# A hybrid encoder block with routed experts on one core: gates read sooner, first gathers spaced, exponentials moved, and VectorE making more low parts

## The reference

```python
def one_block(x_blk):                              # 128 tokens
    q = (x_blk @ w_q).reshape(n, 8, 2, 128)
    s = einsum('nhpc,hpkc->nhpk', q, keys32)
    top_s, top_i = lax.top_k(s, 16)                # 16 of 128 keys, twice
    ...                                            # best 16 of their 16 x 16 sums
    expert_idx = take_along_axis(cand_i, best_c)
    gate = softmax(best_s)
    act = gelu(einsum('nhkd,nd->nhk', expert_u[expert_idx], x_blk))
    return einsum('nhk,nhkd->nd', gate * act, expert_v[expert_idx])
```

## Time and profile before

| what | us |
|---|---|
| median of three runs | 1655.65 |
| the profiled execution | 1660.05 |
| its span | 1658.3 |
| TensorE busy | 1621.8 (98%) |
| VectorE busy | 1288.4 (78%) |
| ScalarE busy | 790.8 (48%) |
| GpSimd busy | 776.4 (47%) |
| granted TensorE clock, mean | 0.996 |
| DMA, mean over the span | 285 GB/s |

### The profile page before, as it was taken

How to read it: one execution, slowest core, us unless ns; L and a number is a source line. 1 busy time by engine, 2 the same in 40 slices (tenths; PEclk the granted TensorE clock), 3 DMA queues, 4 the chain that set the end, 5 groups by cost and what they waited for, 6 DMA issues and landing times.

```text
span 1658.3 us, 26242 instructions
## 1 busy us (share of the span) xinstructions
PE 1621.8 (98%) x10068; PEld 1449.7 (87%) x10068; DVE 1288.4 (78%) x2091; ACT 790.8 (48%) x938; POOL 776.4 (47%) x498
## 2 busy tenths in 40 slices
PE   7999999999998999999999999989999999999998
PEld 6877778889998999999999999988888888888886
DVE  3666622265999989999799689766788998989897
ACT  6454433336554566667667667633323233332323
POOL 4333334446855464444455555433365534453450
PEclk9999999999999999999999999999999999999999
DMA  5222223425649999999999999997999999999993
GB/s 165 77 76 76 76 77 90 121 81 141 191 122 355 379 377 317 345 342 331 356 354 407 417 353 409 386 323 249 362 358 396 395 396 396 395 396 395 396 393 134
DMA packets 247527, 472.81 MB, mean 285 GB/s; under 512 B 13824, under 2 KB 169504, under 8 KB 242080
## 3 DMA queue, kind: packets, MB, share of 16 engines
q1 hardware_dynamic: 173520, 253.52, 43.4%
q0 software_dynamic: 55296, 201.35, 31.6%
q10 hardware_dynamic: 18640, 17.06, 3.0%
HBM read 427.84 MB, written 44.04 MB: 285 GB/s over the span
## 4 chain that ended last, share of the span: by engine, by line
PE 93%; DVE 2%; ACT 2%; DMA 1%; issue 1%; another core or an unknown queue 1%; SPq 0%; ACTq 0%; DVEq 0%
PE psum L1479 31%; PE psum L1402 21%; PE psum L320 16%; PE psum L1381 6%; PE psum L539 5%; PE psum L1432 5%; PE psum L1390 3%; PE psum L394 1%; PE psum L550 1%; DMA dg<-expert_gate 1%; PE psum L381 1%; PE psum L408 1%; ACT uh L1513 0%; DMA acc<-in_x 0%
## 5 line engine op out<-in xcount | busy, mean ns | idle before, releaser
L1640 POOL DMA_INDIRECT ring<-in_expert_u,index x256 | 376.4, 1470 | 398.3 <-DVE ring L1771 328.0
L1771 DVE SCALAR_TENSOR_TENSOR ring<-ring,x 128x1024 f32<-128x1024 f32 x256 | 306.5, 1232 | 48.1 <-DMA ring<-in_expert_u,index 46.3
L1402 PE MATMUL psum<-xnTh,uh 128*128 128x256 f32 x1024 | 300.0, 293 | 9.0 <-DVE ul L1674 7.3
L1479 PE MATMUL psum<-vh,dwh 128*128 128x512 f32 x768 | 298.8, 389 | 0.0
L1479 PE MATMUL psum<-vl,dwh 128*128 128x512 f32 x768 | 298.8, 389 | 0.0
L1479 PE MATMUL psum<-vh,dwl 128*128 128x512 f32 x768 | 298.8, 389 | 0.0
L1402 PE MATMUL psum<-xnTl,uh 128*128 128x256 f32 x1024 | 289.4, 283 | 0.0
L1402 PE MATMUL psum<-xnTh,ul 128*128 128x256 f32 x1024 | 289.4, 283 | 0.0
L1554 ACT ACTIVATE vh<-v_raw 128x4096 fp32r<-128x4096 f32 x31 | 112.7, 3635 | 324.5 <-PE psum L1479 324.0
L1640 POOL DMA_INDIRECT ring<-in_expert_v,index x128 | 168.4, 1316 | 184.2 <-DVE acc L1776 149.6
L273 POOL TENSOR_TENSOR wl<-raw,wh 128x1024 fp32r<-128x1024 f32 x56 | 136.7, 2448 | 227.3 <-ACT wh L629 226.8
(11 more groups left out here) (259 smaller groups left out, 3061.9 us busy)
## 6 DMA issues: line engine op xcount, KB each, us to landing
u_raw<-in_expert_u SPq DMA_DIRECT2D x128, 512.0 KB
v_raw<-in_expert_v SPq DMA_DIRECT2D x30, 2048.0 KB, 13.5
expert_gate<-grid SPq DMA_DIRECT2D x12, 2048.0 KB
dg<-expert_gate SPq DMA_DIRECT2D x32, 768.0 KB, 20.7
raw<-in_w_in SPq DMA_DIRECT2D x40, 512.0 KB, 3.8
expert_act<-hb ACTq DMA_DIRECT2D x128, 128.0 KB
dh<-expert_act SPq DMA_DIRECT2D x32, 512.0 KB
raw<-in_w_q SPq DMA_DIRECT2D x27, 512.0 KB, 4.0
```

What stands on the lines that cost most here:

```text
L1402: last = nc.tensor.matmul(zb[s][:, 0:UT], w[s][:, c, :], x[:, c, 0:UT], start=(c == 0 and i == 0), stop=(c == C - 1 and i == 2))
L1479: last = nc.tensor.matmul(sums[k], w[s][:, j, b * P:(b + 1) * P], v[s][:, j, half * T:(half + 1) * T], start=(first and j == 0 and n == 0) ...
L1640: nc.gpsimd.indirect_dma_start(out=ring[k][:], out_offset=None, in_=tables[x // SLOTS], in_offset=bass.IndirectOffsetOnAxis(ap=numbers[x / ...
L1771: nc.vector.scalar_tensor_tensor(at, at, 1.0, of, ALU.mult, ALU.mult, accum_out=dots[:, k:k + 1]).then_inc(S["row_used"], 1)
```

## The change

It has five parts.

- `BY_VECTOR` holds tiles 65 to 70, 89 to 94 and 113 to 127. `subtracted(n)` counts what ScalarE's low part has to wait for, since tiles are now left out in between. `room(n)` has new weights, small ones from step 62 to 69 and from 87 to 93.
- In `fetch`, gathers 2 to 6 wait for the transposes of tiles 4 to 8.
- In ScalarE's loop the exponentials of steps 22 and 54 stand between that step's high and low part. The gelu of that step stands in the next step, behind its low part.
- SyncE issues `load_acts(0)` within r = 21 (behind the loads of tiles 84 to 87) and `load_gates(0)` within r = 30 (behind those of tiles 120 to 123), with their waits.
- GpSimd's two first casts stand at gathers 205 and 211 for 206 and 215, and VectorE's weights(0, 0) and weights_lo(0, 0) one step earlier.

```diff
-BY_VECTOR = range(114, STEPS)
-FIRST_ROWS_AT, FIRST_WEIGHTS_AT = 206, 215
+BY_VECTOR = (*range(65, 71), *range(89, 95), *range(113, STEPS))
+
+def subtracted(n):
+    return sum(i % 2 == n % 2 and i not in BY_VECTOR for i in range(n + 1))
+
+FIRST_ROWS_AT, FIRST_WEIGHTS_AT = 205, 211
 FIRST_LOWS = (119, 121)
+FIRST_ACTS_AT, FIRST_GATES_AT = 21, 30
...
 def room(n):
-    return sum((9 + 2 * len(SPREAD.get(i, ()))) * (14 if i < 30 else 11 if i < 64 else 12 if i < 110 else 7) for i in range(1, n + 1))
+    return sum((9 + 2 * len(SPREAD.get(i, ()))) * (15 if i < 30 else 13 if i < 62 else 3 if i < 70 else 14 if i < 87 else 3 if i < 94 else 13 if i < 110 else 7) for i in range(1, n + 1))
...
-        load_acts(0, slice(0, 1))
-
-        for out_ in g_out:
-            sp_.wait_ge(out_, (STORES + PRIMED) * 16)
-        load_gates(0, slice(0, 1))
+                if r == FIRST_ACTS_AT:
+                    for stored in h_out:
+                        sp_.wait_ge(stored, (1 + PRIMED) * 16)
+                    load_acts(0, slice(0, 1))
+            if r == FIRST_GATES_AT:
+                for out_ in g_out:
+                    sp_.wait_ge(out_, (STORES + PRIMED) * 16)
+                load_gates(0, slice(0, 1))
...
-            act.wait_ge(ut_sub[s], r + 1)
+            act.wait_ge(ut_sub[s], subtracted(n))
...
                 high(n + 1)
-                if n - 1 in EXPS:
+                if n in EXPS:
+                    exps(*EXPS[n])
+                elif n - 1 in EXPS:
                     nc.scalar.preload_act_table_set("gelu_and_others")
                 if n + 1 not in BY_VECTOR:
                     low(n + 1)
-            gelu(n)
-            if n in EXPS:
-                exps(*EXPS[n])
+            if n - 1 in EXPS:
+                gelu(n - 1)
+            if n not in EXPS:
+                gelu(n)
...
                 pool.wait_ge(S["row_used"], used)
+            if 2 <= x < EARLY:
+
+                pool.wait_ge(ut_full[x % 2], (x + 2) // 2 + 1 + PRIMED)
...
+            elif n == STEPS - 6:
+                weights(0, 0)
             elif n == STEPS - 5:
-                weights(0, 0)
-            elif n == STEPS - 4:
                 weights_lo(0, 0)
```

## The result

The changed kernel takes 1672.82 us, the median of four runs (1670.48 to 1675.21); before takes 1656.43 beside it (four runs, 1655.26 to 1661.1). The ratio is 1.0095, 95% interval 1.0081 to 1.0108: slower by 16 us, 1%. The forecast was 1656.0 in a range of 1645 to 1665, so it missed, and the range with it. The profiled execution of after took 1672.07 us with a span of 1670.3, 12.0 more than that of before.

What follows compares the result with a forecast made beforehand. TensorE bounds the kernel, with VectorE full up to tile 64, its position deciding the forecast. 15.7 - 5.4 - 1.0 - 8.9 = +0.4 on the profiled 1660.05 gives 1660.5, or 1656.0 as a median; range 1645 to 1665.

Steps and rivals of the forecast that it cites:

- VectorE's queue ahead of tile 65: Up to tile 65: VectorE gets there later by added rows and late first rows, leaving TensorE 15.7 us late.
- nine rows at 1.15: Before tile 65's low part: 116 gathered rows due by step 63 instead of 107, costing VectorE 10.3 us.
- the first rows: Gathers 2 to 6, one a step: row 6 arrives 5.6 us later than VectorE wants it.
- Step 116: Earlier fetch and cast on GpSimd bring tile 116's low part in time: 1.0 us gained.
- step 125: With gates loaded sooner, VectorE's wait for them and the slow products after it go: 8.9 us gained.
- The 0.45 for each low part: Each tile whose low part moves to VectorE saves TensorE 0.45 us; 5.4 in all after tile 65.
- the gates arrive in time and hold nothing up: Gates issued four steps sooner land about 4 us before VectorE reaches weights(0, 0); the rival that they fail: chance 0.07.
- the transfers in steps 72 to 86: VectorE falls some 4 us behind, within its slack; nothing is lost there if the transfers keep up.
- rival (c): Transfers bound steps 72 to 86, slower than before, rows land late: 1663 to 1668 us, chance 0.13.
- the baseline: Whole kernel: before's profiled execution, 1660.05, is 4.4 us above the median 1655.65, so 1660.5 becomes 1656.0.
- removing the stall: Steps 4 to 6: fewer gathers at once may bring TensorE forward by up to 5.9 us.
- Exponentials: Steps 22 and 54: moved into ScalarE's wait, they gain 2 x 1.45 = 2.9 us, before tile 65.

Runs made afterwards that it cites:

- the first and the fourth kernel of the first group: First: the changed kernel without the spacing of gathers 2 to 6, 1662.32 us; fourth: before with the sooner gates alone, 1647.05 us.
- the second and the fourth of the second: Second: before with the moved exponentials alone, 1657.02 us; fourth: before with the sooner gates and the moved exponentials, 1649.22 us.
- the fourth chip: Chip of the fourth group of runs, where the changed kernel, unaltered, was timed a second time: 1670.74 us, ratio 1.0016 to before.

## Why the prediction was wrong

**What held.** VectorE's queue ahead of tile 65 (15.7 for a measured 16.3), by its two terms: nine rows at 1.15 (10.3; 9.8 by the run with the old weights) and the first rows (5.6; 6.8 by the lag at step 64 with and without the spacing, 5.9 with before's rows). Step 116 (1.0) and step 125 (8.9 by the forecast and in the trace). The 0.45 for each low part: from step 66 to 70 and from 89 to 94 the lag falls by 1.7 and 2.25. That the gates arrive in time and hold nothing up.

**First miss, 8.2 us (7.76 of lag from step 83 to 89, and the 0.45 that tile 89 saves): the transfers in steps 72 to 86.** The forecast set this at nothing and gave rival (c) 0.13. The mechanism is rival (c)'s, with two differences. The late operation is the one-hot, not tile 89's low part: "it falls 0.3 a step behind, some 4 us, against 6.5 that a one-hot is early" counted VectorE's work but began from a VectorE on time at step 70. It wasn't, since six low parts had just taken 6.9 us of it, and then 8.9 us of waits for rows came. And the demand was taken as a mean over the stretch (421 GB/s against a ceiling seen at 415), where the pause ahead of it should have been read as transfer time thrown away: 297 GB/s from 820 to 845 us, 304 from there to 890. The waits for one-hots are 5.6 of the 8.2; most of the rest is the second miss once more, the lower clock behind the wait of 3.83.

**Second miss, 1.5 us: the clock after the wait at tile 65.** The step was forecast to last its wait and 3.74. The windows of after, in order of time:

```profile
820.00:821.50 1.50, 1.18 (x9) 1.18 (x10) 1.39 (x2) 0.00 (x0) 0.00 (x0) 0.98 1.00 423
821.50:824.70 3.20, 3.20 (x17) 3.20 (x16) 0.00 (x0) 0.00 (x0) 0.00 (x0) 0.50 0.98 410
824.70:840.00 15.30, 15.30 (x133) 15.30 (x132) 7.48 (x9) 6.04 (x9) 1.87 (x2) 1.00 0.79 269
```

TensorE had stood 4.14 us and worked on for about 1; the granted clock is then 0.50, the 1.2 GHz level, for 3.2 us, in which its products start 0.21 us apart for 0.12 at 2.4 GHz. The same stood in the earlier trace rows (5.08 for 2.87) and I charged it at step 125 and not at the wait that I forecast myself; it is named in rival (c) only.

**Third miss, 5 us: the baseline.** These two and smaller terms (0.6 up to tile 65, 0.2 from step 70 to 83, 0.7 from 94 to 112, 0.2 in the down stage) make 11.4 of the 11.6 by which the trace's difference (12.0) exceeds the sum (0.4). The other 5.2 of the 16.8 are that the forecast took 4.4 us off for the median, as if after's profiled execution would lie as far above its own. It lies 0.75 below. Before's has the stall in steps 4 to 6, and three of its four timed runs are 3 to 5 us shorter. That those had no stall, and that this is the difference, is argued, not shown, since they have no trace; the four undisturbed traces with the dense burst (the first and the fourth kernel of the first group, the second and the fourth of the second) bear it out. The forecast counted removing the stall as a possible gain of 5.9, when on such an execution there is nothing to remove, and the spacing's cost stays.

**Direction.** Rival (c) was the right one, at 1663 to 1668. With 8.2 us for its loss of 3, and 1.5 for the 2.2 of slow products that it names, it gives 1665.7 on the forecast's own baseline and 1670.9 on the right one. Its range still lies under the 1672.8 measured, mostly by the baseline. It was given 0.13 because a late VectorE and transfers at their ceiling were weighed as two conditions. They belong together: every low part moved onto VectorE takes the slack that hides late rows (7.3 us lost with them, 2.4 without).

**Exponentials.** Half of the 2.9 came (0.73 a switch, in the step behind, where two gelus stand before the next high part), and before's own one-hots swallow it. The drain that the Trainium skill (ScalarE: Activation LUTs, What ACT_TABLE_LOAD costs) adds to a switch doesn't show here either: the exponential starts 1.30 us after the load began.

```profile
584.25 1.28 ACT L1511 ACT_TABLE_LOAD   x1
585.55 0.40 ACT L1515 ACTIVATE sel<-sel,st 128x128 f32<-128x128 f32 x1
```

## What to carry to other kernels

An engine that is not the bound has slack as a balance carried from step to step, and everything that is put on it (rows, low parts, late transfers) draws on the same balance: add them up along its queue, not each against its own step. A pause in the use of a full ring is a pause in its transfers, so it has to be paid for behind the pause, where the transfers may already be at their ceiling. And take each part of a bundle on its own: one part here gained 10 us, and the others together cost 26 (ratios 0.9941 and 1.0095).

## What the runs showed of the hardware

- Chips differ by 10 us of 1657 on the same kernel, and the traces show a place: ScalarE's instructions start late with an unknown releaser ("remote"), by up to 4.1 us in steps 4 to 6, around the first burst of gathers, and by up to 4.7 later (step 28 of after on the fourth chip). The DMA share over 503 to 523 us is 0.91 to 0.99 in the stalled traces with the dense burst and 0.94 to 0.99 in the quiet ones, so it doesn't tell them apart. What ScalarE waits for isn't shown by any trace and stays open, and so does whether it is the chip or the single execution that decides.
- The ceiling of gathers and loads together was much the same in the kernels read for it: 408 to 418 GB/s at a share of 1.02 to 1.03.
- A wait of TensorE of 4.14 us (after, tile 65) was followed by 3.2 us at a granted clock of 0.50 and cost 1.5 us more; one of 6.64 (before, step 125) cost 2.2 more; one of 2.79 (before with the new weights, step 60) was followed by 5 us at 0.50.
- A cast on GpSimd stretched a VectorE row to 3.51 and 4.74 us for 1.22, and left a low part that reads PSUM and SBUF at 1.23.
